# Placing the memory keys and values as four raw tiles among the norms, the gate and the mixing

## The reference, cut to what matters

```python
x = layer_norm(ALPHA * x + 0.5 * ffn1(x))       # ln1
# mixing: MLA and differential attention on projections of x,
# each expanded (w_up_mla, w_up_diff), gated by sigmoid(x @ w_gate + b_gate),
# added, and multiplied by w_o
x = layer_norm(ALPHA * x + mixed @ w_o)         # ln2
k, v = split(mem @ mem_w_kv)                    # 256 memory tokens, 4 heads of 256
x = layer_norm(ALPHA * x + attention(x @ mem_w_q, k, v) @ mem_w_o)   # ln3
x = layer_norm(ALPHA * x + 0.5 * ffn2(x))       # ln4
```

## Time and profile before

| | us |
|---|---|
| median of 3 runs | 3162.65 |
| lowest and highest | 3162.6, 3168.82 |
| the profiled execution, its own time | 3157.97 |
| its span in the trace | 3156.2 |
| TensorE busy (matmul) | 3008.6 (95%) |
| VectorE busy | 2012.5 (64%) |
| ScalarE busy | 1357.1 (43%) |
| mean granted TensorE clock | 0.98 |

### The profile page before, as it was taken

How to read it: one execution, slowest core, us unless ns; L and a number is a source line. 1 busy time by engine, 2 the same in 40 slices (tenths; PEclk the granted TensorE clock), 3 DMA queues, 4 the chain that set the end, 5 groups by cost and what they waited for, 6 DMA issues and landing times.

```text
span 3156.2 us, 52697 instructions
## 1 busy us (share of the span) xinstructions
PE 3008.6 (95%) x19072; PEld 2674.2 (85%) x19072; DVE 2012.5 (64%) x3581; ACT 1357.1 (43%) x1983; POOL 182.8 (6%) x196
## 2 busy tenths in 40 slices
PE   8999899998999999999999999998998899999998
PEld 8987777897999699898799776987798888888887
DVE  5565644656556655656755664797599866766665
ACT  4443513344345344434344553654446734443433
POOL 0000000000000000000000000000057700000000
PEclk9999999999999999999999999999999999999999
DMA  7564353555555455555365543532443255555554
GB/s 262 187 203 138 102 178 128 173 186 199 187 186 174 170 188 183 185 186 175 129 203 186 190 154 116 169 113 94 147 155 100 63 185 187 187 185 181 178 181 144
DMA packets 140271, 523.73 MB, mean 166 GB/s; under 512 B 15650, under 2 KB 15650, under 8 KB 137312
## 3 DMA queue, kind: packets, MB, share of 16 engines
q1 hardware_dynamic: 134768, 490.79, 47.1%
q0 software_dynamic: 4784, 29.94, 2.5%
q10 hardware_dynamic: 576, 1.05, 0.1%
HBM read 520.65 MB, written 1.06 MB: 165 GB/s over the span
## 4 chain that ended last, share of the span: by engine, by line
PE 75%; DVE 10%; ACT 3%; issue 2%; DMA 0%; ACTq 0%; DVEq 0%; SPq 0%
PE psum L506 69%; PE psum L1733 2%; DVE wpair L477 1%; PE psum L1917 1%; ACT wpair L474 1%; PE psum L655 1%; PE psum L1718 1%; ACT arena L1295 0%; DVE small L2978 0%; PE psum L1278 0%; DVE arena L2957 0%; DVE st L1325 0%; PE psum L1254 0%; DVE xpair L718 0%; DVE arena L2868 0%
## 5 line engine op out<-in xcount | busy, mean ns | idle before, releaser
L477 DVE TENSOR_TENSOR wpair<-ring,wpair 128x1024 fp32r<-128x1024 f32 (+1 forms) x862 | 1044.5, 1220 | 745.7 <-ACT wpair L474 741.8
L506 PE MATMUL psum<-xpair,wpair 128*128 128x256 f32 x11712 | 1475.6, 285 | 22.5 <-DVE wpair L477 12.3
L506 PEld LDWEIGHTS psum<-xpair,wpair 128*128 128x128 f32 x11712 | 1444.6, 193 | 59.6 <-DVE wpair L477 32.5
L474 ACT CAST wpair<-ring 128x1024 fp32r<-128x1024 f32 (+1 forms) x888 | 918.9, 1044 | 822.4 <-PE psum L506 767.7
L506 PE MATMUL psum<-wpair,hpair 128*128 128x512 f32 x3120 | 753.4, 392 | 7.7 <-DVE hpair L930 7.7
L506 PEld LDWEIGHTS psum<-wpair,hpair 128*128 128x128 f32 x3120 | 573.7, 189 | 120.9 <-issue 10.7
L506 PE MATMUL psum<-wpair,xpair 128*128 128x512 f32 (+3 forms) x1728 | 407.1, 395 | 7.6 <-DVE xpair L718 2.5
L506 PEld LDWEIGHTS psum<-wpair,xpair 128*128 128x128 f32 x1728 | 326.3, 195 | 77.4 <-issue 8.5
L905 ACT ACTIVATE small<-psum 128x256 f32<-128x256 f32 x132 | 50.7, 384 | 232.8 <-PE psum L506 232.8
L941 ACT ACTIVATE small<-psum 128x256 f32<-128x256 f32 x92 | 35.4, 384 | 262.2 <-PE psum L506 262.2
L919 DVE TENSOR_TENSOR small<-small,psum 128x256 f32<-128x256 f32 x132 | 55.5, 421 | 137.8 <-ACT small L905 137.8
(11 more groups left out here) (324 smaller groups left out, 1808.3 us busy)
## 6 DMA issues: line engine op xcount, KB each, us to landing
ring<-wstream SPq DMA_DIRECT2D x934, 512.0 KB, 3.3
arena<-rows POOLq DMA_DIRECT2D x18, 1024.0 KB, 5.4
arena<-diag POOLq DMA_DIRECT2D x2, 1728.0 KB, 10.3
arena<-tbuf POOLq DMA_DIRECT2D x2, 1024.0 KB, 7.3
arena<-x_feat ACTq DMA_DIRECT2D x4, 256.0 KB, 7.4
res<-x_tok POOLq DMA_DIRECT2D x1, 1024.0 KB, 7.0
arena<-mem_feat POOLq DMA_DIRECT2D x1, 1024.0 KB, 4.9
arena<-keys POOLq DMA_DIRECT2D x1, 1024.0 KB, 7.6
```

Of the source, the lines that this page charges most:

```text
L474: eng.copy(hi, raw).then_inc(S("w_hi"), 1)
L477: eng.tensor_tensor(wpair[:, 1, o % PAIRS, 0:w], raw, hi.bitcast(F32), ALU.subtract)\
L506: mm = pe.matmul(out_, a[i], b[j], start=start and n == 0, stop=stop_ and last)
```

## The change

`memk` and `memv` become four stages of one raw tile each, `memk0`, `memk1`, `memv0` and `memv1`. Each is placed around the transposes of another step:

- `memk0` at the first norm: two slots, the transposes of ln1, two slots. It uses banks 5 and 4. The later groups of the transposes of ln1 go to banks 0 and 2 instead of 4 and 5 (`EVEN_BANKS`).
- `memk1` behind gate tile 3: two slots, two groups of "o", a slot, two groups, a slot.
- `memv0` behind `upd`: a slot, the wait for `mixed` and two groups of "mix", a slot, two groups, two slots.
- `memv1` behind `wo`: two slots, the transposes of ln2, two slots.

The memory is loaded in ffn0, between the rows `ln1` and `bgate`, into `gb`, a tile that is first used much later; half of the keys is kept there too. ScalarE and VectorE split two slots of `proj`, `upm`, `wo` and `memq` after the x conversion and before the copies out of the raw tile (`keys_out`, `values_out`). With one tile more ahead, the gate's tiles have g = 12 to 15 instead of 11 to 14, so that tile 3 lies in banks 2 and 3 and the wait quoted above is not made.

```diff
     ffn("ffn0")
+    feat("memk0", 1, False)
     tok("proj", KD, (384, 288, 512))
...
     tok("gate", KD, (512,) * 4)
+    feat("memk1", 1, False)
     tok("upm", 4, (512, 512))
     tok("upd", 4, (512, 512))
+    tok("memv0", KD, (512,), False)
     tok("wo", KD, (512, 512))
-    feat("memk", 2, False)
-    tok("memv", KD, (512, 512), False)
+    tok("memv1", KD, (512,), False)
...
+        def memk0_bank(g, t):
+            return psum[:, 5 - t, :]
...
-        def pe_feat(pe, name, src, after=None, middle=None):
+        def pe_feat(pe, name, src, after=None, middle=None, between=lambda i: None, where=None):
...
-        BEFORE_FFN = ["ln3", "n1_0", "n2_0", "n1_1", "n2_1"]
+        EVEN_BANKS = ["ln1", "ln3", "n1_0", "n2_0", "n1_1", "n2_1"]
...
-        memT = region(0, KD, SEQ)
-        mkT = region(2048, KD, SEQ)
+        memT = gb[:, 0:8, :]
+        mkT = [gb[:, 8:12, :], region(3072, 4, SEQ)]
...
             load_row("ln1")
+            pool.dma_start(memT, memT_in).then_inc(S("c_mem"), 16)
             load_row("bgate")
...
-            pool.wait_ge(S("mixed"), 1)
-            pool.dma_start(memT, memT_in).then_inc(S("c_mem"), 16)
...
-            pe_norm(pe, "ln1", res)
+            pe.wait_ge(S("c_mem"), 16)
+
+            def ln1_between(i):
+                if i == 1:
+                    pe.wait_ge(S("trow"), 1)
+                if i == 2:
+                    pe_norm(pe, "ln1", res)
+
+            pe_feat(pe, "memk0", [memT], between=ln1_between, where=memk0_bank)
...
-            pe.wait_ge(S("om_ready"), 1)
-            pe_transpose(pe, "o", pairs(om))
+
+            def o_between(i):
+                if i == 2:
+                    pe.wait_ge(S("om_ready"), 1)
+                    pe_transpose(pe, "o", pairs(om)[0:2])
+                if i == 3:
+                    pe_transpose(pe, "o", pairs(om)[2:4], first=2)
+
+            pe_feat(pe, "memk1", [memT], between=o_between)
...
+            pe_tok(pe, "memv0", of(memT), between=mix_between)
             x_comes("mix")
             pe_tok(pe, "wo", xt)
-
-            pe.wait_ge(S("c_mem"), 16)
-            pe_feat(pe, "memk", [memT])
-            pe_tok(pe, "memv", of(memT))
-            pe_norm(pe, "ln2", res)
+            pe_tok(pe, "memv1", of(memT), between=lambda i: pe_norm(pe, "ln2", res) if i == 2 else None)
...
             act_x(act, "ln1")
+            split.begin("proj", 2)
...
+            keys_out(0)
...
+            act_x(act, "o")
             split.begin("upm", 2)
-            act_x(act, "o")
+            keys_out(1)
...
             act_x(act, "mix")
+            split.begin("wo", 2)
+            values_out(0)
...
-            split.begin("memq")
             act_x(act, "ln2")
+            split.begin("memq", 2)
+            values_out(1)
```

More of the change, by code:

```diff
@@ L626, in pe_feat @@
                 g = s.tile + n
-                if g >= 2:
+                if g >= 2 and where is None:
                     wait_lin(pe, g - 1)
@@ L634, in pe_feat @@
                             x_part(pe, k)
-                            products(pe, bank(g, t)[:, j * SEQ:(j + 1) * SEQ], part(w, slice(k * P, (k + 1) * P)),
+                            products(pe, (where or bank)(g, t)[:, j * SEQ:(j + 1) * SEQ],
+                                     part(w, slice(k * P, (k + 1) * P)),
                                      [x_[:, k, :] for x_ in src], k == 0, k == KD - 1,
```

43 lines of the change are left out of this document (30 added, 13 removed).

## The result

The changed kernel takes 3134.21 us (median of 4 runs, 3132.71 to 3142.23), the kernel before, run beside it, 3164.72 (4 runs, 3162.6 to 3168.82): a ratio of 0.9911, with an interval of 0.9894 to 0.9928. That is 30.5 us less between the medians, 28.4 against the median the prediction started from. Forecast were 3135 us and 27.6 us less. The two profiled executions differ by 25.3 us, 3157.97 against 3132.71.

A forecast was written before the change was run, and what follows sets the result against it. TensorE, busy 95%, was taken to bound the kernel, leaving its stops and low clock to win: 7.9 - 1.0 + 1.4 + 5.4 + 4.7 + 2.9 + 6.3 = 27.6 us, from 3162.65 to 3135 us, range 3127 to 3144.

The forecast's parts named there:

- The stops and what replaces them: TensorE's stops in the first block: tiles placed singly there win 7.9, 5.4, 4.7 and 2.9 us.
- First norm: Before the projection: a raw tile around the norm's transposes, 0.5 us wait left, projection at 215.4, 7.9 us won.
- "o": Between gate tile 3 and upm: the keys' second tile fills the stop, upm 15.6 us after the gate, 5.4 won.
- Mixing: Between upd and wo: a value slot covers the wait for "mixed", 15.5 us instead of 6.5, 4.7 won.
- second norm: Between wo and memq: one tile split around the transposes, memq 16.4 us after wo's end, 2.9 us won.
- Clock: Projection, up stages and wo start at 2.4 GHz once stops are filled: 6.3 us won, ends 0 and 6.3.
- Ring at the projection: Behind the first raw tile, projection slots land late beside GpSimd's bias loads: 1 us of stall, ends 0 and 4.
- Rival B: Ring runs thin behind raw tiles: four places stall about 3 us each, 12 more, 3147 us; chance 0.11.
- Rival C: Ring starvation throughout: slots landing in 12 us cost about 13 us at four places, 3187 us; chance 0.03.
- Gate tile 3: Moves to banks 2 and 3, so its wait for the last attention unit goes: 1.4 us won.
- Rival A: Clock not won back behind the filled stops, or lost again elsewhere: 3141 us; chance 0.10.
- Memory load: Its 1024 KB move to the first burst in ffn0: no cost, hidden by pairs split ahead; at worst 2 us.

The follow-up runs named there:

- clock_only: The kernel before, with 26 unread matmuls on constants in the stops of the first norm, "o" and the mixing, no tile moved; 3156.84 us, ratio 0.9975.
- copies_first: The changed kernel with the copies out of each raw tile placed before the split of the next stage's first two slots; 3145.71 us, ratio 0.9939.
- again: The changed kernel, unaltered, run once more for a second profile; 3136.99 us in one run.
- undo_ln1: The changed kernel with memk0 moved back behind wo and the ln1 transposes in one piece in their old banks; 3148.11 us, ratio 0.9964.
- again_timed: The changed kernel, unaltered, timed beside the kernel before and some variants; 3138.53 us, ratio 0.9920.
- keep_wait: The changed kernel, but gate tile 3 waits for the last attention unit as in the kernel before; 3136.10 us in one run.

## Why the prediction was right

**The stops and what replaces them** held to a few tenths. First norm: forecast 0.5 us of wait and the projection at 215.4; measured 0.18 and 215.90, in an execution whose relative product is 0.68 us late already. Won 8.1 against 7.9. "o": 5.7 against 5.4. Mixing: 7.2 less the 1.9 of the up stages is 5.3 against 4.7; second norm: 5.04 less 1.77 is 3.3 against 2.9. All four were forecast a little too low. `memq` starts 26.0 us earlier than 492.20, inside the 25 to 31 that the prediction named as its test. Taken back one at a time they are worth 7.0, 4.9, 4.2 and 3.1; the first three are lower because a tile returned behind `wo` costs 12.7 and not 13.8 there.

**Clock**: 6.3 in the sum, 6.1 in clock_only (2.0, 2.0 and 2.1). In the changed kernel the up stages and `wo` show 1.9 and 1.8; the projection's part is mixed with its stall, and 0.8 is what the two leave of the forecast 1.2. `wo` and `memq`, each right behind a raw tile, last 0.3 us longer than at full clock elsewhere (22.37 against 22.04, 23.59 against 23.26), at a grant of 1.00 for `wo`; the cause is open.

**Ring at the projection**: 1 us taken out of 0 to 4; 1.0 us measured on average. The bias loads, to which the prediction gave it, make about half. Slots landed in 5.4 us at the median, between the 3.3 and 7.2 of the forecast. Rival B's stops behind the other three tiles did not come: no idle time there is ended by the ring. copies_first shows that there was no room to spare: with the copies first, each of the four places stops for 2 us. Rival C's condition, 10 us of landing, did not occur at the first norm, where a slot took 7.2 us at most.

**Gate tile 3**: 1.4 us in the sum, 1.2 measured (16.05 to 14.86 us, and 16.01 with the wait put back). The mechanism held; what moved is the low stretch, from the products to the tile.

**Rival A** came true in part, and this is the step that the sum lacked. It priced the clock only behind the filled stops and had nothing for a stretch that appears at a stop that was harmless before: 1.6 us at 331, and more where that stretch comes to 3.4 us and not 1.7, as in again. undo_ln1 shows it gone with the first norm's stop back, clock_only shows it come without tiles. Behind `memq` the program is as long as before in the two profiled executions (3156.2 - 492.20 = 2664.0 and 3130.9 - 466.16 = 2664.7 us), though the same code takes 2662.1 to 2671.5 in the other runs, 2667.5 on average. Before has one profile, and that is of an execution 4.7 us below its median, so a loss of a few us behind `memq` is neither shown nor excluded. The sum was 2.3 us too high against the profiled executions (27.6 against 25.3), while the medians of the result differ by 30.5 and those of again_timed by 24.2: that 3135 is met within 1 us is partly luck.

**Memory load**: nothing, as said, though ScalarE's waits became four.

## What to carry to other kernels

Work that depends on nothing recent is worth most when it is cut to the size of the stops: four tiles of 13.8 us in one heap covered one stop, the same four placed singly covered four, and each place must have its first split pairs made before the tile is copied out. Price the clock apart from the idle time, here about 2 us for the stage behind a stop, and expect some of it to be lost again at a later short wait that was harmless before. When a low stretch moves, compare over a span that holds it in both kernels; the length of one stage alone misleads, as it does at gate tile 3. A stop that can't be filled with real work can be filled with matmuls whose results are not read; in nine later norms that gave 9 us between the medians.

## What was not expected of the hardware

A short wait of TensorE is followed by the low clock in one execution and not in another. The wait of 1.3 us at the first attention's end was followed by the full grant before and in undo_ln1, and by 0.50 in eight of nine profiles in which the tile fills the first norm, 115 us earlier, and in clock_only, where other matmuls fill it. In the ninth (keep_wait) the grant stayed 1.00 with the same instructions ahead. The wait of 3.73 us before `memq` left 1.00 before, and 0.50 followed it in clock_only. Over the program, low-clock stretches shift and some are twice as long in one execution as in another (1.7 and 3.4 us by the sum above, at 284 to 292 us); the same code takes 2662 to 2672 us behind `memq`. What decides at which wait the grant falls was not found out.
